# The last inverse level left out of a blockwise triangular solve

## The reference

```
def step(state, inp):
    r_t, w_t, k_t, v_t, kk_t, a_t = inp
    sa = einsum('bhij,bhj->bhi', state, -kk_t)
    state = (state * w_t[:, :, None, :]
             + sa[..., :, None] * (kk_t * a_t)[:, :, None, :]
             + v_t[..., :, None] * k_t[:, :, None, :])
    y = einsum('bhij,bhj->bhi', state, r_t)
    return state, y
```

## Time and profile before

| what | before |
|---|---|
| median of three runs | 2139.3 us |
| profiled execution: its own time | 2141.21 us |
| profiled execution: span | 2139.5 us |
| mean granted TensorE clock | 0.931 |
| TensorE busy | 1903.9 us, 89% |
| VectorE busy | 728.3 us, 34% |
| ScalarE busy | 425.5 us, 20% |
| GpSimd busy | 90.0 us, 4% |
| DMA, mean rate over the span | 216 GB/s |

### The profile page before, as it was taken

The page is one execution under the profiler, slowest core; times in us unless marked ns, Lnnn a source line. Parts: engine busy times, 40 slices in busy tenths (PEclk is TensorE's granted clock), DMA queues, the critical chain, the costliest instruction groups (busy, mean ns, idle before and its releaser), DMA issues.

```text
span 2139.5 us, 23666 instructions
## 1 busy us (share of the span) xinstructions
PE 1903.9 (89%) x9336; PEld 976.3 (46%) x9336; DVE 728.3 (34%) x1221; ACT 425.5 (20%) x848; POOL 90.0 (4%) x120
## 2 busy tenths in 40 slices
PE   6998899999967879999999957978978999999994
PEld 3433688888832433333333323467543333333331
DVE  2189667666633131111111113576113111111112
ACT  3253222222210201111111103244021111111110
POOL 3350000000000000000000010000000000000001
PEclk9998899999967879999999988997878999999997
DMA  8000100000023239999999966210114999999995
GB/s 270 0 0 0 40 1 1 0 0 0 1 79 157 79 122 411 429 429 428 430 428 429 428 245 223 79 40 1 40 40 186 420 429 429 429 429 428 429 428 198
DMA packets 68794, 461.82 MB, mean 216 GB/s; under 512 B 18764, under 2 KB 19910, under 8 KB 44166
## 3 DMA queue, kind: packets, MB, share of 16 engines
q1 hardware_dynamic: 55658, 435.86, 49.3%
q10 hardware_dynamic: 10780, 16.86, 2.2%
q0 software_dynamic: 2304, 8.39, 1.2%
HBM read 442.21 MB, written 18.87 MB: 216 GB/s over the span
## 4 chain that ended last, share of the span: by engine, by line
PE 77%; DVE 13%; ACT 5%; issue 2%; DMA 1%; POOL 0%; ACTq 0%; DVEq 0%; POOLq 0%
PE bank L595 20%; PE bank L613 11%; PE bank L569 10%; PE bank L1822 4%; PE bank L799 3%; PE bank L1714 3%; PE bank L1830 3%; PE bank L878 3%; PE bank L1912 3%; PE bank L577 2%; ACT hT L378 2%; PE bank L1853 2%; PE bank L1838 1%; DVE ring L1635 1%; PE bank L548 1%
## 5 line engine op out<-in xcount | busy, mean ns | idle before, releaser
L595 PE MATMUL bank<-ring,arena 128*64 128x512 f32 x2048 | 450.4, 592 | 1.6 <-DVE arena L453 1.6
L506 DVE TENSOR_TENSOR arena<-arena,bank 64x512 f32<-64x512 f32 x64 | 68.3, 1067 | 646.8 <-ACT arena L386 646.8
L595 PEld LDWEIGHTS bank<-ring,arena 128*64 128x64 f32 x2048 | 146.8, 137 | 293.4 <-issue 291.3
L569 PE MATMUL bank<-xn,arena 128*64 128x512 f32 x1024 | 236.6, 604 | 7.4 <-DVE arena L506 5.0
L613 PE MATMUL bank<-ring,arena 128*64 128x512 f32 x1024 | 236.4, 604 | 0.9 <-ACT arena L390 0.9
L1714 PE MATMUL bank<-hT,ring 128*128 128x512 f32 x336 | 147.6, 599 | 1.1 <-ACT hT L246 0.8
L569 PEld LDWEIGHTS bank<-xn,arena 128*64 128x64 f32 x1024 | 74.4, 140 | 157.3 <-issue 130.8
L613 PEld LDWEIGHTS bank<-ring,arena 128*64 128x64 f32 x1024 | 68.5, 138 | 123.5 <-issue 122.3
L386 ACT ACTIVATE arena<-bank 64x512 f32<-64x512 f32 x64 | 37.8, 590 | 401.2 <-PE bank L595 401.2
L453 DVE TENSOR_TENSOR arena<-bank,gffn 128x512 f32<-128x512 f32 x64 | 44.3, 692 | 189.8 <-PE bank L577 189.8
L1822 PE MATMUL bank<-ring 128*128 128x128 f32 x768 | 101.0, 284 | 4.8 <-DVE ring L1630 3.9
(11 more groups left out here) (309 smaller groups left out, 2017.4 us busy)
## 6 DMA issues: line engine op xcount, KB each, us to landing
ring<-in_moe_w_gate_dram SPq DMA_DIRECT2D x64, 2048.0 KB, 11.4
ring<-in_moe_w_up_dram SPq DMA_DIRECT2D x64, 2048.0 KB, 16.3
ring<-in_moe_w_down_dram SPq DMA_DIRECT2D x64, 2048.0 KB, 13.5
expert_rows<-arena ACTq DMA_DIRECT2D x128, 128.0 KB, 7.8
ring<-in_rec_w_in_dram SPq DMA_DIRECT2D x5, 2048.0 KB, 13.1
ring<-in_att_w_in_dram SPq DMA_DIRECT2D x3, 2048.0 KB, 11.6
ring<-in_rec_w_out_dram SPq DMA_DIRECT2D x2, 2048.0 KB, 10.2
ring<-in_att_w_out_dram SPq DMA_DIRECT2D x2, 2048.0 KB, 19.3
```

What stands on the lines that cost most here:

```text
L506: nc.vector.tensor_tensor(hb[0:CAP, par, :].rearrange("s (f p) -> s p f", f=4), sg[0:CAP, par, :].rearrange("s (p f) -> s p f", f=4), bank ...
L569: mm = nc.tensor.matmul(bank[2][h * CAP:(h + 1) * CAP, :], onehot[:, par, t, :], xn[:, t, h * 512:(h + 1) * 512], start=(t == 0), stop=(t ...
L595: mm = nc.tensor.matmul(bank[par][k * CAP:(k + 1) * CAP, :], xg[:, par, c, :], W[k][:, c * FF:(c + 1) * FF], start=(c == 0), stop=(c == KC ...
```

## The change

The number of levels becomes `NL = LEVELS - 1`, six: the inverse stops at blocks of 64 tokens, and z(6), t(6), the turning behind t(5) and their vector and scalar work are gone. Each chunk of 128 tokens is then solved in two halves of 64: `rhs` makes the right side of the first half alone, `solve` has a call for each half and uses a 64x64 block of the inverse, and a new `carry` between them makes the right side of the second half from the state, v, and the first half's U through M. ScalarE copies right side and U by halves. The steps get new places in TensorE's queue. The preparation parts move from levels 3, 4, 5 to levels 2, 3, 5. The hardware loop over the tiles is written out on all four engines. The counts of the semaphores follow.

```
+        NL = LEVELS - 1
+        halves = lambda d: (slice(d * HD, d * HD + HD), slice(HD - d * HD, P - d * HD))
...
-            with pool.Fori(0, FT - 1) as ft:
+            for ft in range(FT - 1):
...
-            def rhs_copy(ft, d, s):
-                act.wait_ge(rhs_done, 2 * (2 * ft + d) + s + 1)
-                nc.scalar.activation(RU[:, 0, :], bank[6][:, 0:256], ACT.Copy).then_inc(rhs_out, 1)
+            def rhs_copy(ft, d, s, half):
+                hs = halves(d)[half]
+                act.wait_ge(rhs_done, 4 * (2 * ft + d) + 2 * s + half + 1)
+                nc.scalar.activation(RU[hs, 0, :], bank[6][hs, 0:256], ACT.Copy).then_inc(rhs_out, 1)
...
                     turned_copies(*last)
-                    rhs_copy(*last, 0)
-                    u_copy(*last, 0)
-                    output_copies(*last, 0)
-                    rhs_copy(*last, 1)
-                for l in range(1, LEVELS - 1):
-                    if last is not None and l == 2:
-                        output_copies(*last, 1)
...
+                    rhs_copy(*last, 0, 0)
+                    u_copy(*last, 0, 0)
+                    rhs_copy(*last, 0, 1)
+                for l in range(1, NL):
+                    if last is not None:
+                        if l == 1:
+                            u_copy(*last, 0, 1)
+                        if l == 2:
+                            output_copies(*last, 0)
+                        if l == 3:
+                            rhs_copy(*last, 1, 0)
+                        if l == 4:
+                            rhs_copy(*last, 1, 1)
+                        if l == 5:
+                            output_copies(*last, 1)
...
-                    if nxt is not None and l in (3, 4, 5):
-                        if l == 3:
-                            dve.wait_ge(ys_out, 3 * u + 1)
+                    if nxt is not None and l in (2, 3, 5):
+                        if l == 2:
+                            dve.wait_ge(bktok_ready, u)
...
+                        if l == 5:
+                            dve.wait_ge(ys_out, 3 * u + 1)
+                        prepare({2: 0, 3: 2, 5: 4}[l], *nxt)
...
-                    if nxt is not None and l in (3, 4, 5):
-                        prepare(2 * (l - 3) + 1, *nxt)
+                    if nxt is not None and l in (2, 3, 5):
+                        prepare({2: 1, 3: 3, 5: 5}[l], *nxt)
...
                 for b in range(NSEQ):
                     c = 2 * b + cs
                     if s == 1:
-                        nc.tensor.matmul(bank[6][:, b * P:(b + 1) * P], ARt[d][:, c, 0, :], Sst[:, b, :],
+                        nc.tensor.matmul(bank[6][hs, b * P:(b + 1) * P], ARt[d][:, c, 0, hs], Sst[:, b, :],
                                          start=True, stop=False)
                     for h in range(2):
                         i = 2 * b + h
-                        mm = nc.tensor.matmul(bank[6][:, i * HD:(i + 1) * HD], Mb[d][:, 2 * c + h, 2, :],
+                        mm = nc.tensor.matmul(bank[6][hs, i * HD:(i + 1) * HD], Mb[d][:, 2 * c + h, 2, hs],
                                               Vtok[:, c, h * HD:h * HD + HD], start=(s == 0), stop=(s == 0 or h == 1))
                 mm.then_inc(rhs_done, 1)
...
+            def solve(ft, d, s, half):
...
+                u, cs, hs = 2 * ft + d, s if d == 0 else 1 - s, halves(d)[half]
+                if s == half == 0:
+                    pe.wait_ge(t_out, 2 * NL * (u + 1))
+                pe.wait_ge(rhs_out, 4 * u + 2 * s + half + 1)
                 for i in range(4):
                     c, h = 2 * (i // 2) + cs, i % 2
-                    mm = nc.tensor.matmul(bank[6][:, 256 + i * HD:256 + (i + 1) * HD], Tb[d][:, 2 * c + h, 1, :],
-                                          RU[:, 0, i * HD:(i + 1) * HD], start=True, stop=True)
+                    mm = nc.tensor.matmul(bank[6][hs, 256 + i * HD:256 + (i + 1) * HD], Tb[d][hs, 2 * c + h, 1, hs],
+                                          RU[hs, 0, i * HD:(i + 1) * HD], start=True, stop=True)
                 mm.then_inc(u_done, 1)
...
+            def carry(ft, d, s):
...
+                u, cs, (h1, h2) = 2 * ft + d, s if d == 0 else 1 - s, halves(d)
+                pe.wait_ge(u_out, 4 * u + 2 * s + 1)
+                for b in range(NSEQ):
+                    c = 2 * b + cs
+                    if s == 1:
+                        nc.tensor.matmul(bank[6][h2, b * P:(b + 1) * P], ARt[d][:, c, 0, h2], Sst[:, b, :],
+                                         start=True, stop=False)
+                    for h in range(2):
+                        i = 2 * b + h
+                        o = bank[6][h2, i * HD:(i + 1) * HD]
+                        nc.tensor.matmul(o, Mb[d][:, 2 * c + h, 2, h2], Vtok[:, c, h * HD:h * HD + HD],
+                                         start=(s == 0), stop=False)
+                        mm = nc.tensor.matmul(o, Mb[d][h1, 2 * c + h, 0, h2], RU[h1, 1, i * HD:(i + 1) * HD],
+                                              start=False, stop=(s == 0 or h == 1))
+                mm.then_inc(rhs_done, 1)
...
                 if last is not None:
-                    solve(*last, 0)
+                    solve(*last, 0, 0)
...
                 z(0)
                 if last is not None:
-                    outputs(*last, 0)
-                for l in range(1, LEVELS):
+                    carry(*last, 0)
+                for l in range(1, NL):
                     z(l)
-                    if last is not None and l == 1:
-                        rhs(*last, 1)
-                    if last is not None and l == 2:
-                        outputs(*last, 1)
+                    if last is not None:
+                        if l == 1:
+                            solve(*last, 0, 1)
+                        if l == 2:
+                            outputs(*last, 0)
+                        if l == 3:
+                            rhs(*last, 1)
+                        if l == 4:
+                            carry(*last, 1)
+                        if l == 5:
+                            outputs(*last, 1)
                     t(l)
-                    if last is not None and l == 1:
-                        solve(*last, 1)
+                    if last is not None:
+                        if l == 3:
+                            solve(*last, 1, 0)
+                        if l == 4:
+                            solve(*last, 1, 1)
...
             for s in range(2):
                 rhs(FT - 1, 1, s)
-                solve(FT - 1, 1, s)
+                solve(FT - 1, 1, s, 0)
+                carry(FT - 1, 1, s)
+                solve(FT - 1, 1, s, 1)
                 outputs(FT - 1, 1, s)
```

More of the change, by code:

```diff
@@ L1370, in unit_copies @@
                     turned_copies(*last)
[L1371 to L1384 removed]
+                    rhs_copy(*last, 0, 0)
[13 more added lines that the diff above has]
+                            output_copies(*last, 1)
+                    if l < NL - 1:
+                        for q in range(2):
+                            act.wait_ge(t_turned, 2 * (NL - 2) * (2 * ft + d) + 2 * (l - 1) + q + 1)
+                            nc.scalar.activation(Tb[d][:, 4 * q:4 * q + 4, 0, :],
+                                                 bank[4 + q][:, :].rearrange("p (k t) -> p k t", k=4),
+                                                 ACT.Copy).then_inc(t_copied, 1)
+                    if last is not None:
+                        if l == 3:
+                            u_copy(*last, 1, 0)
+                        if l == 4:
+                            u_copy(*last, 1, 1)
                     if nxt is not None and l == 2:
@@ L1387, in _ @@
             unit_copies(0, 0, None, (0, 1))
-            with act.Fori(0, FT - 1) as ft:
+            for ft in range(FT - 1):
                 unit_copies(ft, 1, (ft, 0), (ft + 1, 0))
@@ L1393, in _ @@
             for s in range(2):
-                rhs_copy(FT - 1, 1, s)
-                u_copy(FT - 1, 1, s)
+                for half in range(2):
+                    rhs_copy(FT - 1, 1, s, half)
+                    u_copy(FT - 1, 1, s, half)
                 output_copies(FT - 1, 1, s)
@@ L1604, in masks_and_inverse @@
                                             ALU.mult).then_inc(m_out, 1)
-                for l in range(LEVELS):
+                for l in range(NL):
                     if l == 0:
@@ L1636, in masks_and_inverse @@
                         ins.then_inc(t_out, 1)
-                    if nxt is not None and l in (3, 4, 5):
-                        prepare(2 * (l - 3) + 1, *nxt)
+                    if nxt is not None and l in (2, 3, 5):
+                        prepare({2: 1, 3: 3, 5: 5}[l], *nxt)
             masks_and_inverse(0, 0, (0, 1))
-            with dve.Fori(0, FT - 1) as ft:
+            for ft in range(FT - 1):
                 masks_and_inverse(ft, 1, (ft + 1, 0))
@@ L1865, in products_and_inverse @@
                 if last is not None:
```

(23 more changed lines are left out.)

35 lines of the change are left out of this document (16 added, 19 removed).

## The result

The changed kernel takes 2153.2 us (median of 6 runs, 2152.56 to 2157.75) against 2139.5 for the one before (6 runs, 2136.61 to 2145.18): 1.0064 times, 95% interval 1.0049 to 1.0079. The forecast was 2154. In a second measurement (experiment 5) it took 2155.6 against 2140.8, 1.0060 (1.0042 to 1.0078). Leaving out one of the inverse's seven levels made the kernel 0.6% slower.

The account below looks back on a forecast made before the run. TensorE's in-order queue was taken as the bound. Units 1 to 6 +11.1, unit 0 -3.7, unit 7 +0.8 and the tail +7.1 sum to +15.3 us on the median 2139.3, forecast 2154 us; range 2131 to 2168.

Parts of the forecast that it names:

- the outputs of step 0: Moved from the free gap ahead of z(1) to between z(2) and z(3): 2.50 us, no longer free; that part costs 0.58.
- the carry of step 1: Fill between z(4) and t(4) in each loop unit, priced at 2.75 us including its changes of array form.
- the idle time ahead of the turn: At a unit's end TensorE would idle about 1.8 us for prep_ready, since VectorE's last preparation part comes behind the final additions.
- Rival 1: Not slower: the array takes 64x64 forms in carry and solves without draining; 2136 us with changes at 0; chance 25%.
- the nearest row: Trace row of step 1's outputs, four changes of form at 0.15 us each; taken as the price for the 64x64 form.
- +1.85: Forecast lengthening of one loop unit in us: -0.42 - 1.30 + 0.58 + 4.77 - 1.78.
- The loop: Writing out the hardware loop over the tiles was costed at nothing, from -1.5 us per unit to nothing lost.
- The tail: Serial end of the recurrence: step 0 +3.3, step 1 +3.85, together +7.1 us at full clock, up to +10 at half clock.
- Rival 2: The clock falls in the unit's thin places, before its turn and in the carries: 2189 us; chance 8% (over 2168).
- 1.04 less 8 x 0.05: Start of a loop unit: rhs of step 0 falls from 1.04 to 0.62 us, so z(1) comes 0.42 earlier.
- 2139.3 + 15.3: Median before plus the summed change of the recurrence in us, given as a forecast of 2154.

Follow-up runs that it names:

- experiment 5: The changed kernel measured once more, unaltered, beside the kernel before: 2155.61 us, 1.0060 of the kernel before.
- experiment 2: The kernel before, loop kept, with six levels and preparation at levels 2, 3, 4, leaving out the coupling of a chunk's halves: 2094.62 us, 0.980 of before.
- experiment 4: The changed kernel with the carry's products grouped by form, 3 changes of form instead of 9 in step 1: 2147.37 us, 1.0039 of the kernel before.
- experiment 6: The changed kernel with the state's and v's products of both halves made in rhs, leaving carry four 64-row products: 2149.65 us, 1.0036 of the kernel before.
- experiment 1: The kernel before with its hardware loop written out on four engines and nothing else: 2139.87 us, 0.9998 of before.
- experiment 8: The changed kernel with products that nothing reads in each wait of the tail: 2145.82 us, 1.0022 of the kernel before.
- 9: The kernel before with unread products in the waits of its tail: 2133.02 us, 0.9971 of the kernel before.
- experiment 7: The changed kernel with both halves' state and v products in rhs, every step one place earlier, preparation at levels 2, 3, 4: 2128.87 us, 0.9937 of before.
- experiment 3: The changed kernel with the last preparation part ahead of the final additions instead of behind them: 2152.08 us, 1.0045 of the kernel before.

## Why the prediction was right

**The level's worth and where it went.** The forecast was that the halves cost more than the level gives, and it holds: 45.7 won (experiment 2), 59 given back. The three places named were the right ones: the outputs of step 0 left their free gap (2.29 us between z(2) and t(2), 331.69 to 333.98), the carry of step 1 took 2.49 in the open, and the idle time ahead of the turn came, with the releaser foretold, at 1.52 instead of 1.8 us.

**Changes of form.** Rival 1 turned at 0.02 us per change, and the runs show 0.14: from the starts in the carry, and by taking six of them away (experiment 4). So a change into or out of the 64x64 form costs about what the nearest row gave, 0.15. Each fill came out some 0.1 or 0.2 smaller than priced: counted from the end of the passes ahead of it, the carry of step 1 took 2.58 (priced 2.75), a solve 0.70 (0.78), the outputs of step 0 2.39 (2.50). That is why a unit is +1.47 and not +1.85; levels a little longer than the priced 5.12 took a part of it back.

The Trainium skill, "TensorEngine Tiling (Array Packing)", Tiling Modes, which says that a change of tiling mode drains the engine while different tiles work in parallel, agrees with both halves of this: the 0.14 of experiment 4, and the second half's products that cost nothing in experiment 6.

**The loop.** Costed at nothing, and shown at 0.9998 (0.9986 to 1.0009) by experiment 1.

**The tail, mis-sized.** "Each step gets a carry and a solve with a hop each, ... together +7.1 at full clock" is about right as a difference at one clock: +6.8 by experiments 8 and 9, an estimated 6 without the delays of the unread products themselves. What failed is the bound that the text put on the clock: it let only "the tail's second half" run slow, for "up to +10". In the changed kernel TensorE works 2.50 of the first 4.21 us behind the turn and has half the clock from 601.5, inside the first carry, so that all behind the first solve but two products runs slow: +11.9 (+10.3 in the second profile, where the clock fell a microsecond later and came back for a while). The start of it in the first profile:

```profile
600.93 0.33 PE L1812 MATMUL bank<-arena,ring 128*64 128x64 f32 x2 [0.47 <-ACT arena L1351]
601.19 0.33 PE L1814 MATMUL bank<-arena,ring 64*64 64x64 f32 x2
601.44 0.47 PE L1812 MATMUL bank<-arena,ring 128*64 128x64 f32 x2
```

That the clock falls in the tail was known from the earlier trace rows; that with the new short steps it falls earlier was not worked out.

**Rival 2, the clock in the units.** It didn't happen in the changed kernel (1.00 in all of units 1 to 7), but nearly. It was looked for in the 1.8 us ahead of the turn and in the carries, and it stands elsewhere: in the gap ahead of z(1), when that gap is emptied (experiments 4, 6 and 7). In the changed kernel the long carry of step 0 fills it, so that removing waste there gave nothing back.

**Slips in the working.** They move the sum by under a microsecond. Of the eight units, unit 0 takes 49.66 us and unit 7 45.71, not 46.0 to 46.5. Unit 7 starts at 546.00 and not at the 546.40 of the earlier trace rows, so it is 0.3 shorter than the unit it was set beside, and 0.75 shorter than the other units of its direction. 1.04 less 8 x 0.05 is 0.64, not 0.62, and 2139.3 + 15.3 is 2154.6.

**What the total owes to luck.** The loop units came out 2.3 us below the forecast, the tail 4.8 above, and stages behind it, which the forecast moved as a block, varied by several microseconds with their own clock: the recurrence is 17.4 and 16.6 us longer in the two profiles, the median 13.7 and 14.8. 2153.2 beside 2154 is closer than the terms are. The stated range, 2131 to 2168, was wide enough to hold rival 1 and no change at all; the terms say more than the hit.

## What to carry to other kernels

When a level is dropped from a chain of products, price each step that takes its place where it will stand, and ask which of the old ones lay free in a gap. Before work is taken out of a gap on TensorE, look at the granted clock of the stretch behind it: here work saved inside the gap of step 0's carry did not bring z(1) forward, and went with spells at half clock that cost a unit a microsecond or more; five unread products took them away. In a serial tail, compare at one clock first, then ask when the clock falls.

## What the hardware showed that was not expected

- A single spell at half clock, of 3 to 4 us, can hit a unit that is some 94% busy on TensorE: it costs about 1.3 us and shows as one z(1) of 3.3 to 3.7 us instead of 2.36 and a mean clock of 0.96. In experiments 3, 4 and 7 it stood on z(1), right behind the gap. Idle time directly ahead of z(1) of 0.51 us went with none in the seven units of each of three profiles (the changed kernel's two and experiment 8), 1.35 with 2 of 7 (experiment 4), 1.96 with a clock below 1.00 in all 7 (experiment 6). It isn't a rule: experiment 7 has 6 of 7 at 0.82, where a wait of 0.47 stands close before, and experiment 3 has one such unit at 0.51. What decides between units of one kernel stays open.
- Layer 1's attention, with the same 949 passes, took 272.9 to 279.0 us from one profile to another, at clock 0.91 to 0.88. A few microseconds of any comparison of these kernels come from there; what sets it was not tried.
- The half clock of the tail reaches past it. With the tail filled, the group norm and what follows up to the output projection took 52.3 to 52.5 us instead of 54.3 to 56.4.
